# First block of a two-layer transformer kernel: the first unit's low part ahead of w_ada's products, the forget gates' logits in another bank, shift columns and normalising at other steps

## The reference

```python
mod = jax.nn.silu(c) @ w_ada + b_ada                      # 1024 -> 6 x 1024
shift_m, scale_m, gate_m, shift_f, scale_f, gate_f = jnp.split(mod, 6, axis=-1)
h = rmsnorm(x, g_mix_pre) * (1.0 + scale_m[:, None]) + shift_m[:, None]
z = h @ w_in                    # q, k, v, fl (8 forget gates), pool, conv, gates
log_f = jax.nn.log_sigmoid(f_logit.astype(jnp.float32))   # f_logit = fl + b_f
cum_f = jnp.cumsum(log_f, axis=1).transpose(0, 2, 1)
logits = jnp.einsum('bhqd,bhkd->bhqk', qb, kb).astype(jnp.float32) * scale
logits = logits + cum_f[:, :, qs:qe, None] - cum_f[:, :, None, :qe]
p = jax.nn.softmax(logits, axis=-1).astype(v.dtype)       # causal, 8 heads of 64
merged = gates[:, :, 0] * (br_a @ wa) + gates[:, :, 1] * (br_b @ wb) + gates[:, :, 2] * (br_c @ wc)
```

## Time and profile before

| | |
|---|---|
| runs | 840.93, 843.23, 843.15 us; median 843.15 |
| profiled execution | 842.49 us |
| its span, first to last instruction | 841.2 us |
| mean granted TensorE clock | 0.986 |
| busy: PE, PEld | 799.8 us (95%), 725.4 us (86%) |
| busy: DVE, ACT, POOL | 561.7 (67%), 415.8 (49%), 84.8 us (10%) |
| chain that ended last: PE, DVE, ACT | 82%, 7%, 6% |

### The profile page before, as it was taken

How to read it: one execution, slowest core, us unless ns; L and a number is a source line. 1 busy time by engine, 2 the same in 40 slices (tenths; PEclk the granted TensorE clock), 3 DMA queues, 4 the chain that set the end, 5 groups by cost and what they waited for, 6 DMA issues and landing times.

```text
span 841.2 us, 13025 instructions
## 1 busy us (share of the span) xinstructions
PE 799.8 (95%) x5300; PEld 725.4 (86%) x5300; DVE 561.7 (67%) x761; ACT 415.8 (49%) x610; POOL 84.8 (10%) x129
## 2 busy tenths in 40 slices
PE   2999999999999999999999999899999999999995
PEld 2888888989879999999989998688987999999994
DVE  5776878869966555656665889847556665555573
ACT  4435365753446454445456477457544544444441
POOL 6200980001110000000001000011000100000000
PEclk8899999999999999999999999999999999999998
DMA  9978977767544655655556544445534465656641
GB/s 306 352 232 254 368 246 247 249 245 268 195 158 151 196 181 177 196 177 180 195 177 193 177 156 151 127 149 195 171 108 129 136 199 191 196 180 192 185 150 50
DMA packets 83323, 163.70 MB, mean 195 GB/s; under 512 B 5424, under 2 KB 13808, under 8 KB 83264
## 3 DMA queue, kind: packets, MB, share of 16 engines
q1 hardware_dynamic: 81344, 157.31, 57.3%
q10 hardware_dynamic: 1424, 4.81, 1.7%
q0 software_dynamic: 496, 0.76, 0.3%
HBM read 161.81 MB, written 1.05 MB: 194 GB/s over the span
## 4 chain that ended last, share of the span: by engine, by line
PE 82%; DVE 7%; ACT 6%; issue 3%; POOL 1%; DMA 1%; SPq 0%; ACTq 0%; DVEq 0%; POOLq 0%
PE bank L1631 25%; PE bank L1632 24%; PE bank L1633 24%; DVE lo_ring L864 2%; ACT hi_ring L461 2%; DVE ada_acc L896 2%; PE bank L1805 1%; PE bank L1675 1%; PE bank L2135 1%; PE bank L2156 1%; DVE x_residual L969 1%; DMA ada_ring<-in_w_ada 1%; ACT gates L516 1%; PE bank L1809 1%; PE bank L1824 1%
## 5 line engine op out<-in xcount | busy, mean ns | idle before, releaser
L864 DVE TENSOR_TENSOR lo_ring<-raw_ring,hi_ring 128x1024 fp32r<-128x1024 f32 x248 | 305.6, 1237 | 187.1 <-ACT hi_ring L461 186.2
L461 ACT CAST hi_ring<-raw_ring 128x1024 fp32r<-128x1024 f32 x248 | 258.7, 1049 | 296.0 <-PE bank L1633 283.3
L1631 PE MATMUL bank<-h_hi,hi_ring 128*128 128x256 f32 x1008 | 291.4, 289 | 2.4 <-DVE h_lo L928 1.5
L1632 PE MATMUL bank<-h_lo,hi_ring 128*128 128x256 f32 x1008 | 285.8, 284 | 0.0
L1633 PE MATMUL bank<-h_hi,lo_ring 128*128 128x256 f32 x1008 | 285.7, 283 | 0.0
L1631 PEld LDWEIGHTS bank<-h_hi,hi_ring 128*128 128x128 f32 x1008 | 194.0, 192 | 6.9 <-issue 4.1
L1632 PEld LDWEIGHTS bank<-h_lo,hi_ring 128*128 128x128 f32 x1008 | 194.1, 193 | 0.9 <-issue 0.2
L1633 PEld LDWEIGHTS bank<-h_hi,lo_ring 128*128 128x128 f32 x1008 | 193.9, 192 | 0.0
L1631 PE MATMUL bank<-hi_ring,branch_hi 128*128 128x512 f32 x320 | 125.8, 393 | 0.1
L1632 PE MATMUL bank<-lo_ring,branch_hi 128*128 128x512 f32 x320 | 124.7, 390 | 0.0
L1633 PE MATMUL bank<-hi_ring,branch_lo 128*128 128x512 f32 x320 | 124.6, 389 | 0.0
(11 more groups left out here) (263 smaller groups left out, 944.5 us busy)
## 6 DMA issues: line engine op xcount, KB each, us to landing
raw_ring<-in_w_ff SPq DMA_DIRECT2D x128, 512.0 KB, 3.7
raw_ring<-in_w_in SPq DMA_DIRECT2D x64, 512.0 KB, 4.5
raw_ring<-in_w_out SPq DMA_DIRECT2D x16, 512.0 KB, 3.6
raw_ring<-in_w_xkv SPq DMA_DIRECT2D x16, 512.0 KB, 3.7
mem_v<-in_w_ada SPq DMA_DIRECT2D x12, 512.0 KB, 6.6
ada_ring<-in_w_ada SPq DMA_DIRECT2D x10, 512.0 KB, 5.4
mem_k<-in_w_ada SPq DMA_DIRECT2D x10, 512.0 KB, 5.6
raw_ring<-in_w_branch SPq DMA_DIRECT2D x8, 512.0 KB, 5.2
```

Source lines behind the costliest of these rows:

```text
L461: act.copy(m.hi[:, m.slot(u)], m.raw[:, m.slot(u)]).then_inc(s.hi_done, 1)
L864: dve.tensor_tensor(m.lo[:, m.slot(u)], m.raw[:, m.slot(u)], as_f32(m.hi[:, m.slot(u)]), ALU.subtract).then_inc(s.lo_done, 1)
L1631: pe.matmul(out, a_hi, b_hi, start=start, stop=False, skip_group_check=True)
L1632: pe.matmul(out, a_hi, b_lo, start=False, stop=False, skip_group_check=True)
```

## The change

Five edits, all in the first block.

- VectorE, start: lo(0) and the first quarter's `affine_lo` come directly behind `norm_columns(0, 0)`, and two of w_ada's products, which stood ahead of them, behind. lo(0) also comes ahead of `affine_lo`.
- TensorE and VectorE: the forget logits are made and read in bank 4 instead of bank 0.
- ScalarE: `normalize` of step at + 2 is no longer behind the unit's cast but at the head of the step, ahead of the sigmoids (where the step has them) and of the cast. That is steps 7, 12, 17 and 23.
- TensorE: `ff_shift` lies beside unit GATES + 18 (c = 4, j = 2, step 22) instead of GATES + 16 (step 20).
- VectorE: the matching `ada_columns` comes behind GATES + 18 instead of GATES + 17.

```diff
--- before.py
+++ after.py
@@ -592,12 +592,15 @@
         for g, at in enumerate(ATT1_AT):
             if step == at + 1:
                 exponentials(s.att1, g, m.soft1[g])
-            if step == at + 2:
-                normalize(s.att1, g, m.soft1[g])
             if step == at + 4:
                 take_turned(s.att1, g, 6, m.turned1[g])
             if step == at + 5:
                 attended_hi(s.att1, g, 6, g)
+
+    def normalize1(step):
+        for g, at in enumerate(ATT1_AT):
+            if step == at + 2:
+                normalize(s.att1, g, m.soft1[g])
 
     for j in range(RING):
         if j == RING - 1:
@@ -607,6 +610,7 @@
     for c in range(6):
         for j in range(RING):
             i = RING * c + j
+            normalize1(RING + i)
             if j == RING - 1:
                 act.wait_ge(s.used, GATES + i + 1)
                 if c == 3:
@@ -1040,10 +1044,10 @@
     for _ in range(KD):
         ada()
     norm_columns(0, 0)
+    lo(0)
+    affine_lo(s.xm, (0,))
     for _ in range(UK):
         ada()
-    affine_lo(s.xm, (0,))
-    lo(0)
     for q in range(RING - 1):
         u = RING * q
         for _ in range(UK):
@@ -1084,7 +1088,7 @@
     dve.wait_ge(s.fl_ps, 1)
     dve.wait_ge(s.small_in, SMALL_LOADS * DMA)
     for tt in range(NT):
-        ins = dve.tensor_tensor(m.fl[:, tt, :], bank[0][:, tt * NH:tt * NH + NH], m.bf_row[:, :], ALU.add)
+        ins = dve.tensor_tensor(m.fl[:, tt, :], bank[4][:, tt * NH:tt * NH + NH], m.bf_row[:, :], ALU.add)
     ins.then_inc(s.fl_out, 1)
     dve.wait_ge(s.fl_out, 1)
     flz = m.fl[:, :, :].rearrange("p a h -> p (a h)")
@@ -1133,7 +1137,7 @@
             i = RING * c + j
             attention1(RING + i)
             after(GATES + i)
-            if c == 4 and j == 1:
+            if c == 4 and j == 2:
                 ada_columns(s.ff_shift_ps, s.ff_shift, 0, 8, 16, 24)
             if c == 2 and j == 1:
                 ada_row(s.gate_row_ps, s.mix_rows_in, s.gate_row, m.rows[:, 0, :], 0)
@@ -1746,15 +1750,15 @@
     def forget_logits(i):
 
         if i == 0:
-            claim(0)
+            claim(4)
             pe.wait_ge(s.small_in, SMALL_LOADS * DMA)
         tt = i // 4
         for k in (2 * (i % 4), 2 * (i % 4) + 1):
-            mm = pe.matmul(bank[0][:, tt * NH:tt * NH + NH], m.h_f32[:, k, tt * P:tt * P + P], m.w_fl[:, k, :],
+            mm = pe.matmul(bank[4][:, tt * NH:tt * NH + NH], m.h_f32[:, k, tt * P:tt * P + P], m.w_fl[:, k, :],
                            start=(k == 0), stop=(k == KD - 1), skip_group_check=True)
         if i == 7:
             mm.then_inc(s.fl_ps, 1)
-            free[0] = s.fl_out, 1
+            free[4] = s.fl_out, 1
 
     def cumulative():
 
@@ -1897,7 +1901,7 @@
         for j in range(RING):
             i = RING * c + j
             features(GATES + i, j, m.h_hi, m.h_lo, b0,
-                     beside=ff_shift if (c, j) == (4, 0) else scores1(RING + i))
+                     beside=ff_shift if (c, j) == (4, 2) else scores1(RING + i))
             attention1(RING + i)
             if c == 2 and j == 1:
                 pe.wait_ge(s.ada_used, 24)
```

## The result

The changed kernel takes 844.93 us (median of 12 runs, 843.67 to 845.68); the kernel before, in the same sessions, 842.97 (12 runs, 840.93 to 845.82). The ratio is 1.002, with an interval from 1.0011 to 1.003: slower by about 1.7 us, where 842.0 was forecast with a range to 844.8. The profiled execution took 843.87 us, 1.1 under its median, with a span of 842.6.

What follows compares the result with a forecast made beforehand. TensorE's matmuls, covering 95% of the span, were taken to bound the kernel. The terms -1.15 - 0.33 - 0.55 + 1.0 + 1.2 gave +0.2 us, or -1.3 with the clock kept; forecast 842.0 us, range 838.3 to 844.8.

Steps and rivals of the forecast that it cites:

- Start: lo(0) and affine_lo ahead of two w_ada products: first matmul at 18.6 instead of 19.75, gain 1.15 us.
- the cap of 1.65: Upper end of the gain at the start: the second unit, begun at 25.0, can't begin before lo(1) ends at 23.3.
- Forget logits: Bank 4 removes a wait before MIX_B's first unit: gain 0.33 us, or 1.8 if the clock stays up.
- Pair 0: Step 7, early scalings: transposes' stall goes, copy ends at 123.5, just before TensorE wants it; gain 0.55, 0.2 possibly lost.
- Pair 1: Early scalings with a long step 15 before the products with v: no stall before or after, nothing gained or lost.
- Pair 2: Step 17, columns moved from step 20 to 22: lo 2.6 us late, attend(2) waits for the copy; net +1.0 us.
- Pair 3: Step 23, early scalings: stall of 0.56 goes, but the late copy holds attend(3) until 191.05; net +1.2 us.
- The sum: All terms together: +0.2 us if the half-clock stretch stays, -1.3 if it goes; 842.0 put between 842.7 and 841.2.
- The new waits don't come: Rival, 20%: VectorE's copies don't wait behind the late lo's, all stalls are pure gain; 837.1 to 839.1 us.
- The new gaps lower the clock: Rival, 12%: idling at attend(2) and attend(3) brings half-speed stretches of 1.7 us; 844.4 for one, 846.1 for both.

Runs made afterwards that it cites:

- e9: Only the new order at the start, on the kernel before: 841.68 us, ratio 0.9994.
- e3: Only the scalings moved to the head of the step, on the kernel before: 852.58 us, ratio 1.0131.
- e10: Only the forget logits' move to bank 4, on the kernel before: 842.38 us, ratio 1.0001.
- e11: The changed kernel with the scalings of the pair normalised in step 7 alone back behind the cast: 843.82 us, ratio 1.0016.
- e6: The changed kernel with the add of the shift's columns ahead of VectorE's after(GATES + 18), freeing bank 0 earlier: 844.25 us, ratio 1.0031.
- e7: The changed kernel with the pooling product in bank 2 instead of bank 7: 845.13 us, ratio 1.0028.
- e1: The changed kernel with all scalings back behind the cast; start, bank and columns as changed: 840.76 us, ratio 0.9976.
- e4: The new order at the start and the forget logits' bank only, on the kernel before: 841.23 us, ratio 0.9982.
- e5: Only the shift's columns in step 22 and their add behind GATES + 18, on the kernel before: 841.80 us, ratio 0.9987.
- e8: The changed kernel with bank 0 freed earlier and ScalarE's order cast, scalings, sigmoids in steps 7 and 23, old order elsewhere: 837.51 us, ratio 0.9942.
- e2: The changed kernel with the shift's columns back in step 20 and their add a step earlier than changed: 856.31 us, ratio 1.0144.

## Why the prediction was wrong

The direction was missed: 1.15 under the median of 843.15 was forecast, and it came out 1.7 to 2.0 above the kernel before. Two steps failed. At pair 0 the copy was said to fit behind the late lo ("It just fits, because step 10 is long"), a gain of 0.55; it did not fit. At pair 2 the lateness was followed to VectorE's copy alone, while two other paths that hang on the same lo ended later. The terms one by one:

- **Start**: -1.15 forecast, -0.97 at the first matmul and -1.68 at unit 15's end in this pair of traces, the latter a little over the cap of 1.65. Part of that is luck: on average over the traces named above the new order has its first matmul 0.6 us earlier, and the earlier full speed of this trace is not its doing. In the median of the start alone (e9) it is 0.8, and 0 is just inside its interval.
- **Forget logits**: -0.33 taken, -1.8 kept as the end. All ten traces of kernels with bank 4 keep full speed there, three of the four with bank 0 fall to half behind it. Unit 16's last sum comes 4.81 or 4.82 us behind the last logit matmul wherever the clock stays, and 6.26 to 6.28 where it falls: a gain of 1.47, with the wait of 0.31 for minus_log_f, as worked out. e3, with bank 0, its stall of 0.33 and the clock kept, also has 4.81: the stall by itself costs nothing there, since without it the sums wait for minus_log_f. But the bank alone (e10) moved no median.
- **Pair 0**: this is the first step that failed. -0.55 forecast, +1.87 in the trace (from -3.15 to -1.28), +1.1 by e11. With the shift of 3.15 my 123.5 for the copy's end becomes 120.35; it ended at 121.19, and TensorE waited 1.04. The term stood on durations from one execution and a margin of 0.07 us. VectorE's small scaling of the maxima took 0.69 us where it had taken 0.17, which put the reciprocals 0.5 late, and from the lo to the copy it was 5.66 us instead of 5.39. Then came the half-speed stretch that I had priced only for pairs 2 and 3. Without it the changed order is still 0.35 us slower than the old one at attend(0) (e6 and e7 against e11, from unit 16's last sum), where 0.55 of gain was forecast. Pair 1 was forecast at nothing and has no wait.
- **Pair 2**: this is the second. The lateness of the lo (2.6 us) was right: it came at 157.05, 1.31 later than before where the rest stood 1.28 earlier, so 2.59. But it also delays the read that frees bank 7, and line 1152 with `mixers_br` 2, for which ScalarE waits ahead of its table load, sigmoids and copy. Neither path is in the prediction. In place of 1.8 us at attend(2) TensorE waited 1.84 for bank 7 and 0.65 for ScalarE's copy; attend(2) came 0.0 instead of 0.9 us earlier than before, measured against the step-14 shift of -1.28. The columns' 1.9 us in step 22 came out at 1.67 (that unit takes 4.55 us, where it took 2.88).
- **Pair 3**: +1.2 forecast. From attend(2) to attend(3) it takes 26.81 us in the changed kernel and 25.73 in e1, so +1.1. The wait at attend(3) was forecast at 1.75 and measured 0.99, since a wait of 0.63 for bank 0 at step 24, which I had called nothing, took part of it. e6 shows that the two go together: with the bank freed earlier the other is 1.88.
- **The sum** said +0.2 with the half-speed stretch staying, and I went to 842.0 for the chance that it would go. It was laid on the profiled execution's 842.49, 0.5 under the median of 842.97 of the kernel before, which is 0.5 of the 2.9 that were missed. On the medians: e4 -1.3 and e5 -0.9 against the kernel before, e1 with both -1.8 to -2.0, and the early scalings on top of that +4.2. The waits explain the 4.2: 1.04 + 0.99 for VectorE's copies, 1.84 for bank 7 and 0.65 for ScalarE's copy are 4.5, less the stall of 0.5 that they replace. The way from unit 16's last sum to attend(3) says the same: 103.5 us in e1, 107.5 in e6 and e7, and 109.0 in the changed kernel's trace, whose half-speed stretch is the other 1.5.
- **Rivals**: "The new waits don't come" fell; only e8 reaches its times, by taking the waits away. "The new gaps lower the clock" named the right danger at the wrong place: none of the traces with the columns in step 22 has a half-speed stretch behind attend(2) or attend(3), while three of the six with pair 0's scalings early have 3.4 us of it behind attend(0). That the time came out near its 844.4 is chance. With the columns in step 20 and the scalings early, in e2 and e3, the clock is the larger part of the loss.

## What to carry to other kernels

An instruction moved to the head of a step on an in-order queue brings its own wait with it: ask what that wait stands behind, and follow everything queued after it, bank frees included, not only the next consumer. What the queue needs to do for others (here the cast) goes first into the time that the wait would take. A margin of less than half a microsecond, worked out from one trace, is no margin, and idle time next to sparse matmuls should be priced with what the clock may do behind it.

## What was not expected of the hardware

- Short waits of 2.4 to 2.5 us in all at pair 2 cost about what they last when full slabs follow (the changed kernel, e7, e11). With 1.8 and 1.3 us of waits and small matmuls behind them, the granted clock was 0.50 for 10.2 us in e3 and 23.9 us in e2, through slabs that were dense again, and half of that time was lost.
- ScalarE's table load ran well ahead of its sigmoids in step 15 (138.94 against 144.92) and behind the wait for VectorE in step 19 (160.93, idle 1.73 before it). The program waits once ahead of the sigmoids of step 15 and twice ahead of those of step 19.
- VectorE's scaling of 128x4 elements at pair 0 took 0.69 us instead of 0.17. In eleven of the fourteen traces it began within 0.1 us of GpSimd's operation on pad_u (103.32 to 104.06 here), took 0.68 to 0.69 and ended within 0.04 us behind it. In the three others (before, e5, e9) unit 16 ran at half speed, the scaling fell behind that operation, and it took 0.17. No experiment pulled the two apart, so that GpSimd is the reason is likely and not shown.
